# A two-layer streaming encoder step on one core: four small loads of the second stage issued in the first stage, and layer C's first activations loaded in two halves

## What is computed

```python
def ab_mixer(x, ...):                 # layer 0
    h = rms_norm(x, rms_g)
    q_a, k_a, v_a, glow, z_a, q_b, k_b, v_b, z_b = _split(h @ w_in, SPLIT_AB)
    o_a, S = gla_scan(q_a, k_a, v_a, g_a, S0)                        # gated linear attention
    o_b = swa_sample(q_b, k_b, v_b, k_cache, v_cache, sink, table)   # window attention, cache for the sample
    return x + concat(o_a, o_b) @ w_out, ...

def c_mixer(x, ...):                  # layer 1, "layer C"
    h = rms_norm(x, rms_g)
    z, xbc, dt = _split(h @ w_in, SPLIT_C)
    xbc, new_conv = causal_conv(xbc, conv_state, conv_w, conv_b)
    y, S = ssd_scan(xs, Bm, Cm, softplus(dt + dt_bias), A, S0)
    return x + norm(y * silu(z)) @ w_out, ...
```

## Time and profile before

| | us |
|---|---|
| three timed runs | 2947.81, 2952.59, 2952.68 (median 2952.59) |
| the profiled execution | 2951.21 |
| its span, first to last instruction | 2949.3 |
| first loop begins / second loop begins / layer C begins (first load issued) | 22.2 / 517.3 / 1170.3 |
| PE's mean granted clock over the span | 0.966 of full speed |

### The profile page before, as it was taken

One profiled execution on the slowest core, in us unless ns is written; L12 is line 12 of the kernel. 1 busy time (PEld: TensorE's weight loads), 2 busy tenths in 40 slices (PEclk: granted clock), 3 DMA queues, 4 the chain that ended last, 5 costly groups with the idle time before them and its releaser, 6 DMA issues. The chain is left out here.

```text
span 2949.3 us, 44784 instructions
## 1 busy us (share of the span) xinstructions
PE 2759.3 (94%) x16290; PEld 2312.1 (78%) x16290; DVE 1729.2 (59%) x4127; ACT 1275.1 (43%) x2618; POOL 45.6 (2%) x165
## 2 busy tenths in 40 slices
PE   6999998799999995899989999899999999599999
PEld 3789997477887884788877888688877888378887
DVE  3344434545555554488887888788887888631111
ACT  4455554534444443245454555444454555420000
POOL 0000000100000000000000000000000000000000
PEclk9999999899999997899999999899999999799999
DMA  4222121432333324433335333433344332232321
GB/s 183 94 91 84 74 86 72 132 101 105 113 110 118 114 91 160 132 101 100 98 92 148 89 91 97 138 92 100 101 122 128 91 100 73 99 113 85 114 85 58
DMA packets 272057, 307.87 MB, mean 104 GB/s; under 512 B 49943, under 2 KB 206106, under 8 KB 269754
## 3 DMA queue, kind: packets, MB, share of 16 engines
q1 hardware_dynamic: 269938, 300.73, 32.2%
q10 hardware_dynamic: 1992, 5.48, 0.5%
HBM read 221.85 MB, written 84.30 MB: 104 GB/s over the span
## 5 line engine op out<-in xcount | busy, mean ns | idle before, releaser
L2189 PE MATMUL bank<-h_high,region 128*128 128x256 f32 (+1 forms) x3072 | 591.8, 293 | 8.7 <-DMA h_low<-h1T_low_d 8.5
L2189 PEld LDWEIGHTS bank<-h_high,region 128*128 128x128 f32 x3072 | 489.5, 191 | 47.0 <-issue 29.9
L2189 PE MATMUL bank<-h_low,region 128*128 128x256 f32 (+1 forms) x1536 | 437.5, 285 | 0.0
L2189 PEld LDWEIGHTS bank<-h_low,region 128*128 128x128 f32 x1536 | 292.5, 190 | 0.0
L2011 DVE SCALAR_TENSOR_TENSOR conv_acc<-u,convw,conv_acc 128x256 f32<-128x256 f32 (+1 forms) x576 | 247.2, 485 | 25.7 <-ACT conv_acc L1894 23.3
L2180 PE MATMUL bank<-wz_high,h_high 128*128 128x512 f32 (+1 forms) x544 | 224.7, 413 | 5.4 <-DVE region L2105 4.6
L2404 PE MATMUL bank<-region,yT_high 128*128 128x512 f32 (+1 forms) x544 | 212.9, 391 | 5.0 <-DVE wout_c_low L2386 5.0
L2180 PE MATMUL bank<-wz_high,h_low 128*128 128x512 f32 (+1 forms) x544 | 216.8, 399 | 0.0
L2180 PE MATMUL bank<-region,h_high 128*128 128x512 f32 (+1 forms) x544 | 216.4, 398 | 0.0
L738 PE MATMUL bank<-region,hT_high 128*128 128x512 f32 (+5 forms) x544 | 189.9, 349 | 12.1 <-DVE wa_low L595 12.1
L738 PE MATMUL bank<-wa_low,hT_high 128*128 128x512 f32 (+5 forms) x544 | 187.0, 344 | 0.0
(11 more groups left out here) (298 smaller groups left out, 5977.5 us busy)
## 6 DMA issues: line engine op xcount, KB each, us to landing
h_high<-h1T_high_d SPq DMA_DIRECT2D x64, 512.0 KB, 5.9
h_low<-h1T_low_d SPq DMA_DIRECT2D x64, 512.0 KB, 6.8
acb<-acT SPq DMA_DIRECT2D x64, 512.0 KB, 3.9
yT<-yT_t SPq DMA_DIRECT2D x64, 256.0 KB, 3.6
yT_in<-yT SPq DMA_DIRECT2D x16, 1024.0 KB, 5.4
xin<-in_x_prompt SPq DMA_DIRECT2D x16, 512.0 KB, 3.6
h0T_high_d<-hT_high SPq DMA_DIRECT2D x16, 512.0 KB, 2.6
h0T_low_d<-hT_low SPq DMA_DIRECT2D x16, 512.0 KB, 3.5
```

The lines of the kernel that those rows point to most:

```text
L2189: ins = M(out, wt[:, k, col:col + P], y[h.par][:, k, h.h0:h.h0 + h.n], start=(k == 0 and p == 0), stop=(k == KT - 1 and p == 2))
```

## The change

The four loads of `kdup`, `vprev` and `wdt` move from the start of the second loop into the first loop, between the store of tile 1's h and `next_weights`. Their tiles are allocated for both loops, and their semaphore now belongs to the whole program. In layer C, `first_pair` loads h of the first pair in two halves of the contracted dimension: six loads for slices 0 to 3 on `h_in0`, then six for slices 4 to 7 on a new semaphore, `h_rest`. The state's load stands behind both. PE starts the first slot when the first half is there, and waits for `h_rest` at slice 4. The transposes of the state on PE and its copy on DVE move to the end of their `start`.

```diff
@@ layer_gla, SP: start
                 store_h(n)
+                sp.dma_start(w["kdup"][:, :, 0, :], a["cache_swa_k"][0, 0]).then_inc(c["kcache_in"], 16)
+                sp.dma_start(w["kdup"][:, :, 1, :], a["cache_swa_k"][0, 0]).then_inc(c["kcache_in"], 16)
+                sp.dma_start(w["vprev"][:, :], a["cache_swa_v"][0, 0].rearrange("r k e -> r (k e)")).then_inc(c["kcache_in"], 16)
+                sp.dma_start(w["wdt"][:, :, :], a["w_in_c"][0].rearrange("(k p) n -> p k n", p=P)[:, :, DTC:DTC + HC]).then_inc(c["kcache_in"], 16)
                 next_weights()
@@ layer_swa, SP: start (the same four loads leave)
                 load_kv(x)
-                sp.dma_start(kdup[:, :, 0, :], ...
-                sp.dma_start(kdup[:, :, 1, :], ...
-                sp.dma_start(vprev[:, :], ...
-                sp.dma_start(wdt[:, :, :], ...
@@ layer_c, SP
+            def first_pair():
+                for k, sem in ((0, s["h_in0"]), (4, s["h_rest"])):
+                    for t, col, R in ((0, 0, DEC), (1, DEC, P), (2, DEC + P, P)):
+                        for dst, src in ((hh, d["h1h"]), (hl, d["h1l"])):
+                            sp.dma_start(dst[0][:, k:k + 4, col:col + R].bitcast(F32),
+                                         src[t].rearrange("p (k r) -> p k r", k=KT)[:, k:k + 4, 0:R]).then_inc(sem, 16)
             def start(first):
+                first_pair()
                 first_state(0)
-                load_pair(1, 0, True)
                 load_ac(first, None)
                 load_pair(3, 1, False)
@@ layer_c, DVE: start
-                first_state(0)
                 gate_weights_low(0)
                 ...
                 gate(first)
+                first_state(0)
@@ layer_c, PE: slot
                     if h.first and i == 0:
                         pe.wait_ge(c["x_low"], KT * h.g + k + 1)
+                        if k == 4:
+                            pe.wait_ge(s["h_rest"], 96)
```

More of the change, by code:

```diff
@@ L167, in program @@
         d["yT"] = nc.dram_tensor("yT", [NT, P, DI // P, P], F32).ap()
-        for n in "wc_in wx_in wz_in0 wz_in1 x_high x_low".split():
+        for n in "kcache_in wc_in wx_in wz_in0 wz_in1 x_high x_low".split():
             c[n] = nc.alloc_semaphore(f"c_{n}")
@@ L176, in program @@
             w = {"region": region}
+            w["kdup"] = sb("kdup", [P, KVH, 2, HD], ab)
+            w["vprev"] = sb("vprev", [P, KVH * HD], ab)
+            w["wdt"] = sb("wdt", [P, KT, HC], ab)
             w["raw_b"], w["wout_low"] = two_views(nc, ab, "wb_raw", "wout_low_ab", [P, KT, DM])
@@ L868, in layer_swa @@
         bias = sb("bias", [P, HB, 2 * P])
-        wdt = sb("wdt", [P, KT, HC])
+        kdup, vprev, wdt = w["kdup"], w["vprev"], w["wdt"]
         wh, wl = [w["region"][1][:, i * KT * DM:(i + 1) * KT * DM].rearrange("p (k n) -> p k n", k=KT) for i in range(2)]
@@ L885, in layer_swa @@
         sqk = sb("sqk", [P, P])
-        kdup = sb("kdup", [P, KVH, 2, HD])
         kz = sb("kz", [P, KVH, 2, 2 * P])
         vcur = sb("vcur", [P, KVH * HD])
-        vprev = sb("vprev", [P, KVH * HD])
         sc = sb("sc", [P, HB, 2 * P])
@@ L897, in layer_swa @@
         dtok = sb("dtok_t", [P, 2 * HC])
-        s = names(nc, "swa", """wo_in0 wo_in1 wo_in2 wo_in3 wo_in4 wo_in5 wo_in6 wo_in7 bias_in bias_made bprev_out bprev_in wdt_made w_high w_low kcache_in h_in kv_in oa_in x1_in fin_out x1_out hT_out dt_out
+        s = names(nc, "swa", """wo_in0 wo_in1 wo_in2 wo_in3 wo_in4 wo_in5 wo_in6 wo_in7 bias_in bias_made bprev_out bprev_in wdt_made w_high w_low h_in kv_in oa_in x1_in fin_out x1_out hT_out dt_out
             act_q act_p act_n act_dt dve_q dve_k dve_m dve_d dve_n dve_dt
@@ L962, in start @@
                 load_kv(x)
[L963 to L966, removed]
                 flat = d["skew"].rearrange("q h m -> (q h m)")
@@ L1024, in _ @@
                                     band.unsqueeze(1).to_broadcast([P, HB, 2 * P]), ALU.add).then_inc(s["bias_made"], 1)
-            pool.wait_ge(s["kcache_in"], 64)
+            pool.wait_ge(c["kcache_in"], 64)
             for k in range(KT):
@@ L1585, in start @@
             def start(x, n):
-                pe.wait_ge(s["kcache_in"], 64)
+                pe.wait_ge(c["kcache_in"], 64)
                 for j in range(KVH):
@@ L1676, in layer_c @@
         st = sb("st_c", [P, 8])
-        s = names(nc, "c", """zw_high zw_low h_in0 h_in1 ac_in s0_in
+        s = names(nc, "c", """zw_high zw_low h_in0 h_in1 ac_in s0_in h_rest
             act_norm dve_conv dve_y dve_w dve_norm pool_chain pool_step tail_set
```

## The result

| | before | changed |
|---|---|---|
| median of the timed runs (20 each), us | 2949.94 | 2955.7 |
| ratio, 95% interval | 1 | 1.0014, 1.0008 to 1.002 |
| span of the profiled execution, us | 2949.3 | 2954.7 |
| span of a second profile of each, us | 2948.5 | 2953.7 |

The change makes the kernel about 4 us slower (0.0014 x 2950; the interval is 2.4 to 5.9 us, and the two medians differ by 5.8), where 2.1 us faster was forecast. Three stages answer to the three terms of the prediction. Times of the changed trace are us from the start of its span; its second loop begins at 519.4 (517.3 before), layer C's first load is issued at 1177.6 (1170.3 before).

What follows compares the result with a forecast made beforehand. Inside its loops the kernel was taken as bound by PE, so PE's start of each stage counts. First loop +2.4, second loop -1.8, layer C -2.7 gave -2.1 us against 2951.2: 2949.1 us, range 2945.0 to 2954.0.

Steps and rivals of the forecast that it cites:

- three terms of the prediction: First loop +2.4 us for the added loads, second loop -1.8 us without them, layer C -2.7 us with h first.
- SP's four free slots (2.7 us): Second loop: removing four loads from SP's queue brings the bias 2.7 us earlier, claimed to matter to nobody.
- three signs of being wrong: x not late; layer C's second h wait ending after 13 us; ACT reading queries 12 us or more after DVE's low weights began.
- First loop, +2.4: First loop: four loads ahead of x delay PE 2.0 us, plus 0.4 for the clock; between +0.9 and +3.5.
- the 0.4 for the clock: First loop: PE resumes later, so work before the clock's fall may run at half speed; 0 to 0.8 us, taken 0.4.
- upper end of 3.5: First loop, rival of dearer loads: delay 2.7 us plus clock 0.8, total 2950.2 us; chance 0.15.
- Second loop, -1.8: Second loop: PE starts earlier without waiting for `wdt`, and ACT gets the queries earlier; 1.8 us gained.
- bounds of -0.5 and -1.9: Second loop: gain only 0.5 us if h lands near 523.5; at most 1.9, since DVE's low weights limit the queries.
- Layer C, -2.7: Layer C: h ahead of the state ends the slots 3.0 us earlier, less 0.3 on DVE; between -4.6 and +1.3.
- 0.222 MB per us: Layer C: DMA rate for state and h; first half of h lands 5.3 us after 1171.5, all at 1182.1.
- slower by the halves: Layer C rival: SP's issue sets the pace, rest of h lands 4.0 us later, total 2953.1 us; chance 0.15.
- The sum: Whole kernel: +2.4 - 1.8 - 2.7 = -2.1 us against the profiled 2951.2, giving 2949.1 us.

Runs made afterwards that it cites:

- loads behind x: Changed kernel with the four loads behind tile 2's `load_x`: 0.9998 against before with POOL's add behind tile 0's keys; 0.9987 in both kernels with all repairs.
- the three freed: Changed kernel with POOL's add behind DVE's eighth low-weight product (1.0 against before), and two that also cut the add, move the loads and alter layer C (both 0.9987).
- whole loads: Layer C's h in six whole loads, state behind: on the kernel before with only layer C's part, 0.9995; in the changed kernel with add and loads repaired, 0.9987.
- layer C alone: Kernel before with only layer C's part of the change, h in halves and the state behind; the four loads stay: 0.9987 (0.9976 to 0.9997).
- the loads alone: Kernel before with only the four loads moved into the first loop, layer C as before: 1.0021 (1.0011 to 1.003), 6.2 us slower.

## Why the prediction was wrong

**The step that failed** is this one: "SP's four free slots (2.7 us) bring the bias earlier, which nobody waits for here." Nobody waits for the bias, but POOL does more with it sooner. Before, and in the second profile of before, the last low-weight product had started (528.1) when POOL's add began (528.55); POOL then waited, and its add shows 5.34 us where 4.54 to 4.63 are its own. With the loads gone from SP's queue the add begins 8.6 to 9.7 us after the loop's start instead of 11.2 to 11.3, ahead of the eighth product or, in two of the three traces, of the seventh, which then waits until the add ends: 5.54 - 1.28 = 4.3 us. The rows of before could have shown it: 2.7 us sooner, the add would begin at 525.9, ahead of the product that started at 528.1. Two of the prediction's three signs of being wrong came: ACT read the queries 15.5 us after DVE began its low weights (12 was the mark), and the second wait for h ended 13.07 us after the first load (13). The experiments show this cause from both sides: taken away by a wait or by cutting, made without the change by an order of loads.

**First loop, +2.4: right at its last tile, too small at its end.** At ACT's read of the last x (454 us) five traces with the loads ahead of the weights are 1.42, 2.18, 2.30, 3.27 and 3.31 us later than before, mean 2.5; six without them lie between -0.65 and +0.53. With the loads behind x it is -0.01 to +0.75. The close match is in part luck: ACT's wait for x of tile 2 grew by 2.4 us in the mean where 2.0 was forecast, and the 0.4 for the clock does not show beside it. From there to the second loop's start it is 62.0 to 63.1 us in the six traces without the loads, but 64.1 to 65.0 in six of the eight that have them in the first loop, ahead of the weights or behind x (62.0 and 62.4 in the other two). So with the loads ahead of the weights the second loop begins 3.7 us later in the mean (the first trace of before is the latest of the six), more than the forecast's upper end of 3.5. In the traces the difference lies in how early the clock falls in the loop's last products; whether the loads cause that, and how, is open.

**Second loop, -1.8: the gain had the right size, but the hold took it back and more.** Freed of the hold, softmax is at 37.3 to 37.4 instead of 39.0 and 39.1, so 1.5 to 1.8 us are won (39.0 and 39.1 are before's two profiles). With the hold it is 42.6 to 43.9: 3.6 to 4.8 lost. Both last: up to layer C's first load the second loop takes 654.6 to 658.2 us in the four traces with the hold, 650.5 to 653.2 in the five that are as before there, and 650.8 to 651.1 in the three freed (means 657.0, 652.5, 651.0). My bounds of -0.5 and -1.9 left no room for that.

**Layer C, -2.7: wrong in size, by the traces.** The step was that h moves at 0.222 MB per us however it is cut, so that all of it lands 11.85 us after the first load. With whole loads 12.15 and 12.33 are near that; with twelve loads it is 13.86 in the mean. That is close to the point named for the rival "slower by the halves" (1184.2, 13.95 us after the first load), and the gain at the third slot is 24.62 - 24.51 = 0.1 us. PE's early start on the first half was there, but it only moved 12 products ahead of a wait whose end did not move. The timing does not decide this size: layer C alone timed 0.9 to 7.1 us faster, which contains 2.7, though its trace ends only 0.3 us earlier.

**The sum** with the measured sizes is +2.5, +3.6 to +4.8, -0.1: 6.0 to 7.2. The two changed traces are 6.5 and 7.2 us later in layer C's first tile than the first trace of before. They end 5.4 and 4.4 us later, and timing says 4.1. The rest lies at the ends of layer C's groups, where the granted clock falls for some us, not equally long. Windows there, before and then with layer C's part alone:

```profile
1560.00:1575.00 15.00, 14.20 (x62) 9.72 (x61) 10.49 (x30) 3.61 (x9) 0.00 (x0) 0.80 0.97 286
```

```profile
1560.00:1575.00 15.00, 14.18 (x43) 8.96 (x42) 9.63 (x28) 2.28 (x7) 0.00 (x0) 0.57 1.02 294
```

At that boundary this second trace goes from -0.5 to +2.3 us against before; at three others it wins 1.8, 1.4 and 1.5. Kernels with each of the three forms of layer C's start (state first, whole h, halves) show this jump, 2.4 to 3.0 us; before's second profile and the loads alone do not. Before's second profile differs from the first by up to 1.7 us at the two later boundaries. What decides it stays open.

## What to carry to other kernels

When loads leave a queue, ask what every load behind them will now start, on all engines, and what that will run beside; an instruction nobody waits for can still stand in another's way. Long POOL instructions that read SBUF belong where DVE has nothing urgent, or cut into pieces of about half a microsecond (here 1.0 us of DVE's time instead of 4.3). A busy time that is several times the usual one for the same instruction can be a wait: look at the minimum, median and maximum of a group, not its sum alone.

## What was not expected of the hardware

A POOL add of 128x2048 elements (4.5 us of its own) held one DVE instruction with two SBUF inputs for 4.3 us in four traces, and was itself held by one that had begun first. The page "SBUF — State Buffer" of the Trainium skill, section "SBUF: two separate sides", states this rule: between a DVE instruction with two SBUF inputs and a GpSimd one that reads SBUF, the port pair that the two engines share is an exclusive lock, taken for the whole instruction by whichever starts first. The runs agree with it: 5.54 us for a product of 1.28. By an estimate from the add's 4.5 us, reading it for POOL's add would have put a loss of about 4 us into the second loop's term.

Also held was DVE's TENSOR_SCALAR of 32x8 values (2.51 us instead of 0.16), while TENSOR_REDUCE ran at 0.67 us beside the add as it did without it. Twelve loads of half size landed 1.6 us later than six (13.86 and 12.24 us in the mean). Single issues took up to 2.17 us of SP with the halves and up to 2.30 with whole loads, so a long issue alone does not make the difference.
